# A gather of four experts for 32 tokens in a PEER layer, and two routers moved into the stretches with gathers

## The reference

```
q = (x @ wq).reshape(N, 8, 2, 128)                 # 8 heads
s = einsum('nhpd,hpkd->nhpk', q, keys)             # 128 keys a half
top_s, top_i = top_k(s, 16)                        # per half, then over all 16 x 16 sums
best_s, best = top_k(top_s[0] + top_s[1], 16)
expert = i1 * 128 + i2                             # 16 experts a head, 128 a token, of 16384
gate = softmax(best_s)
a = gelu(einsum('tkd,td->tk', u_tab[expert], x))
y = einsum('tk,tkd->td', gate * a, v_tab[expert])
```

## Time and profile before

| | |
|---|---|
| median of three runs | 5940.83 us |
| profiled execution | 5949.21 us, span 5947.1 us |
| busy: TensorE, VectorE, ScalarE, GpSimd | 4117.5, 2900.9, 1697.3, 1441.5 us |
| moved by DMA | 1712.65 MB, of it 1342.26 MB by GpSimd's queue |
| gathers | 1280 |
| matmul records of the sums (L774) | 10240, busy 1564.5 us |
| dots (L2020) | 1280, busy 1552.5 us |

### The profile page before, as it was taken

One profiled execution on the slowest core, in us unless ns is written; L12 is line 12 of the kernel. 1 busy time (PEld: TensorE's weight loads), 2 busy tenths in 40 slices (PEclk: granted clock), 3 DMA queues, 4 the chain that ended last, 5 costly groups with the idle time before them and its releaser, 6 DMA issues.

```text
span 5947.1 us, 63889 instructions
## 1 busy us (share of the span) xinstructions
PE 4117.5 (69%) x22248; PEld 2506.1 (42%) x22248; DVE 2900.9 (49%) x6835; ACT 1697.3 (29%) x4733; POOL 1441.5 (24%) x1295
## 2 busy tenths in 40 slices
PE   3889477889886685548476677778468785545555
PEld 1677454566563443224132235677335453211111
DVE  0321747544438544664445444322854445654444
ACT  0200137332432342233322222201152442222222
POOL 0000022212221232223343341000023332235443
PEclk7779789969997897778788888669778898767777
DMA  6434367748886798679999995024378997689998
GB/s 257 151 130 162 121 248 281 290 170 319 329 343 234 302 420 328 266 274 386 379 409 411 394 420 200 27 67 155 117 286 361 369 402 318 256 335 421 407 417 358
DMA packets 259315, 1712.65 MB, mean 288 GB/s; under 512 B 37712, under 2 KB 39344, under 8 KB 71600
## 3 DMA queue, kind: packets, MB, share of 16 engines
q0 software_dynamic: 184320, 1342.26, 56.4%
q1 hardware_dynamic: 74672, 366.31, 16.6%
HBM read 1690.43 MB, written 17.92 MB: 287 GB/s over the span
## 4 chain that ended last, share of the span: by engine, by line
PE 42%; DMA 24%; DVE 15%; ACT 6%; issue 4%; DVEq 4%; POOL 3%; ACTq 2%; SPq 1%; PEldq 0%; PEld 0%; POOLq 0%
PE psum L423 25%; DMA arena<-in_uv,arena 21%; PE psum L774 10%; DVE arena L2020 3%; POOL arena L1108 3%; DVE arena L1932 1%; DVE arena L1925 1%; DMA arena<-in_w_ada 1%; DVE arena L1926 1%; PE psum L383 1%; PE psum L604 1%; PE psum L605 1%; ACT arena L1444 1%; ACT arena L1441 1%; PE psum L639 1%
## 5 line engine op out<-in xcount | busy, mean ns | idle before, releaser
L1108 POOL DMA_INDIRECT arena<-in_uv,arena x1280 | 1437.6, 1123 | 4469.9 <-PE psum L774 3039.1
L774 PE MATMUL psum<-arena 64*64 64x512 f32 x10240 | 1564.5, 742 | 1086.5 <-ACTq L1445 990.9
L2020 DVE CUSTOM_DVE_ANT_0 arena<-arena 128x1024 f32<-128x1024 f32 x1280 | 1552.5, 1226 | 1330.0 <-DMA arena<-in_uv,arena 1272.4
L423 PE MATMUL psum<-arena 128*128 128x256 f32 (+2 forms) x8480 | 1945.9, 388 | 171.4 <-DVEq L1464 120.4
L423 PEld LDWEIGHTS psum<-arena 128*128 128x128 f32 (+1 forms) x8480 | 1616.9, 195 | 599.2 <-issue 194.1
L774 PEld LDWEIGHTS psum<-arena 64*64 64x64 f32 x10240 | 392.7, 157 | 2068.6 <-ACTq L1445 1375.8
L1438 ACT ACTIVATE arena<-arena 128x2 f32<-128x2 f32 x640 | 130.9, 205 | 1684.8 <-DVEq L2022 1671.3
L1444 ACT ACTIVATE arena<-arena 128x64 f32<-128x64 f32 x1280 | 376.2, 340 | 45.8 <-issue 1.8
L383 PE MATMUL psum<-arena 128*128 128x128 f32 (+1 forms) x680 | 129.4, 346 | 337.3 <-DVE arena L1523 119.8
L1441 ACT ACTIVATE arena<-arena 128x1 f32<-128x1 f32 x1280 | 307.6, 287 | 45.5 <-issue 1.3
L383 PEld LDWEIGHTS psum<-arena 128*128 128x128 f32 (+1 forms) x680 | 97.9, 178 | 391.2 <-issue 183.5
(11 more groups left out here) (210 smaller groups left out, 2747.4 us busy)
## 6 DMA issues: line engine op xcount, KB each, us to landing
arena<-in_w_in SPq DMA_DIRECT2D x92, 1024.0 KB, 5.9
arena<-in_w_mix SPq DMA_DIRECT2D x120, 768.0 KB, 7.3
arena<-in_w_ada SPq DMA_DIRECT2D x32, 1536.0 KB, 16.4
arena<-in_w_wq SPq DMA_DIRECT2D x40, 1152.0 KB, 6.0
arena<-in_w_wo SPq DMA_DIRECT2D x20, 1024.0 KB, 7.5
arena<-in_uv,arena POOLq DMA_INDIRECT x1280, 10.8
arena<-ada_rows SPq DMA_DIRECT2D x15, 512.0 KB, 5.6
arena<-x_rows SPq DMA_DIRECT2D x14, 512.0 KB, 6.2
```

The lines of the kernel that those rows point to most:

```text
L423: ins = mm(out, a, b, start=(i == 0), stop=(i == last))
L774: ins = mm(psum[o, r_ * 512:r_ * 512 + 512], DIAG[rows, c, :], RING[rows, sl, D + half * 512:D + (half + 1) * 512], start=first, stop=last ...
L1108: pool.indirect_dma_start(RING[:, sl, :], None, io["uv"], bass.IndirectOffsetOnAxis(IDX[:, t, h * TOPK + k:h * TOPK + k + 1], 0)).then_inc ...
L2020: V_.tensor_tensor_reduce(out=RING[:, sl, 0:D], in0=RING[:, sl, 0:D], in1=XT[:, u % 2, :], scale=1.0, scalar=0.0, op0=ALU.mult, op1=ALU.ad ...
```

## The change

A gather now brings, to partition 32e + i, an expert of token i of 32 tokens: four experts each (e = 0 to 3) for 32 tokens. A unit is half a tile, 64 tokens as two sets of 32, with 32 groups of two gathers; there are 20 units. Since the partitions no longer stand for tokens one by one, the picks of a head go through DRAM: VectorE writes numbers and gates to `PICK`, SyncE stores them to `pick_rows`, waits, and loads them in four pieces into `PICKED` (`hand_over`); GpSimd and ScalarE wait for `picked`. The token rows are loaded four times over into `XT`, one buffer for each set of 32, by ScalarE's queue. `QUAD`, four stacked 32x32 identities, takes the place of `PAIR`, and the sum has four matmuls of 128x32 and 256 columns, one for each quarter of the width, in two PSUM banks that alternate by unit. `route` of layer 0 pair 0 and of layer 1 pair 1 moves to the head of the next segment, with cost 28 a head, and `quotas` holds back items whose head isn't handed over.

```
-GROUPS = PH * TOPK // GS
+TG = 32
+SUB, PER = P // TG, TOPK * TG // P
+HG = 2 * PER // GS
+GROUPS = PH * HG
...
-        return [12.0] * PH
+        return [(28.0 if (l, pairs) in OVERLAPPED else 12.0)] * PH
-UNITS = [(0, t) for t in range(NT)] + [(1, t) for t in range(CT, NT)]
+OVERLAPPED = ((0, (0,)), (1, (1,)))
+UNITS = [(0, t, f) for t in range(NT) for f in range(2)] + [(1, t, f) for t in range(CT, NT) for f in range(2)]
...
+                if st[0] == "route" and n < PH - 1:
+                    want = max(done, min(want, routed_upto(items, st[1], st[2], n - 1)))
...
-        PAIR = view(keep(64), [64])
+        QUAD = view(keep(TG), [TG])
...
+        def acc_bank(u):
+            return psum[:, (u % 2) * 512:(u % 2) * 512 + 512]
...  TensorE
-                if g == 0 and u:
-                    pe.wait_ge(s("acc_out"), u)
+                if g == 0 and u >= 2:
+                    pe.wait_ge(s("acc_out"), u - 1)
-                    for half in range(2):
-                        for r_ in range(2):
-                            rows, o = slice(64 * r_, 64 * r_ + 64), slice(64 * (half ^ r_), 64 * (half ^ r_) + 64)
-                            ins = mm(psum[o, r_ * 512:r_ * 512 + 512], DIAG[rows, c, :], RING[rows, sl, D + half * 512:D + (half + 1) * 512],
+                    for q in range(4):
+                        ins = mm(acc_bank(u)[32 * q:32 * q + 32, gg * 256:gg * 256 + 256], DIAG[:, c, :], RING[:, sl, D + q * 256:D + (q + 1) * 256],
...  SyncE
+                def hand_over(h):
+                    n = PH * r + h
+                    sp.wait_ge(s("gated"), n + 1)
+                    rows = pick_rows[n]
+                    sp.dma_start(rows.rearrange("(t p) c -> p t c", p=P), PICK[:, h % 2]).then_inc(s("pick_out"), 16)
+                    sp.wait_ge(s("pick_out"), 16 * (n + 1))
+                    if n:
+                        sp.wait_ge(s("picked"), 64 * n)
...
+                    for e in range(4):
+                        src = rows[:, 2 * PER * e:2 * PER * (e + 1)].rearrange("(g p) c -> p g c", p=TG)
+                        sp.dma_start(PICKED[r % 2][TG * e:TG * (e + 1), h], src).then_inc(s("picked"), 16)
                 for h in range(PH):
                     chunks(1)
+                    if h:
+                        hand_over(h - 1)
+                    if h == PH - 1:
+                        hand_over(h)
                     yield
...  ScalarE
+            def load_xt(u, gg):
+                l, t, f = UNITS[u]
+                xt[gg] += 1
+                at_ = t * P + 64 * f + TG * gg
+                for e in range(4):
+                    act.dma_start(XT[TG * e:TG * (e + 1), gg, :], h2_rows[at_:at_ + TG, :]).then_inc(s(f"xt_in{gg}"), 16)
...
+                if u + 1 < len(UNITS) and (UNITS[u + 1][0], UNITS[u + 1][1] // 2) in h2_ready:
+                    if g == GROUPS - 1 - HG // 2:
+                        load_xt(u + 1, 0)
+                    if g == GROUPS - 1 and xt[1] == u + 1:
+                        load_xt(u + 1, 1)
```

More of the change, by code:

```diff
@@ L129, in schedule @@
+    e1 = [("route", 1, (1,)), ("q", 1, (2,)), ("da", 1, (2,)), ("ml_on", 1, both), ("mc", 1, (2,)), ("mln", 1, (2,)), ("merge", 1, (2,)), ("route", 1, (2,))]
+    p0 = sequence(range(0, 4))
+    p1 = sequence(range(4, 12))
+    p2 = sequence(range(12, 20))
+    cut = 4 * GROUPS
     return [(a, [], 0), (b, p0, 0), (c1, p1[:cut], 0), (c2, p1[cut:], 8), (d, [], 0), (e1, p2[:cut], 0),
-            ([("final", 2, ())], p2[cut:cut + GROUPS], 8), ([("final", 3, ())], p2[cut + GROUPS:cut + GROUPS + 16], 8),
@@ L131, in schedule, with routed_upto @@
-            ([("final", 4, ())], p2[cut + GROUPS + 16:], 16), ([("final", 5, ())], [], 0)]
+            ([("final", 2, ())], p2[cut:cut + 64], 8), ([("final", 3, ())], p2[cut + 64:cut + 80], 8),
+            ([("final", 4, ())], p2[cut + 80:], 16), ([("final", 5, ())], [], 0)]
 SEGMENTS = schedule()
 PSEQ = [item for _, items, _ in SEGMENTS for item in items]
+def routed_upto(items, l, pairs, heads):
+    for i, item in enumerate(items):
+        if item is not None:
+            (ul, t, _), g = UNITS[item[0]], item[1]
+            if (ul, (t // 2,)) == (l, pairs) and g // HG >= heads:
+                return i
+    return len(items)
@@ L145, in quotas @@
             row = []
-            for cost in steps(*st):
+            for n, cost in enumerate(steps(*st)):
                 cum += cost
                 want = lead + int(round((len(items) - lead) * cum / total))
+                if st[0] == "route" and n < PH - 1:
+                    want = max(done, min(want, routed_upto(items, st[1], st[2], n - 1)))
                 row.append(want - done)
@@ L351, in slots, with route_of, picked_by, picks @@
         def slots(u, g):
[L353 to L354 removed]
+            first = u * GROUPS * GS + g * GS
+            return [(n, n % RS, n % 16, g // HG, (g * GS + i) // PER % 2, (g * GS + i) % PER) for i, n in enumerate(range(first, first + GS))]
         ROUTES = [(l, pairs[0]) for stages, _, _ in SEGMENTS for kind, l, pairs in stages if kind == "route"]
[L358 to L360 removed]
+        def route_of(u):
+            l, t, _ = UNITS[u]
+            return ROUTES.index((l, t // 2))
+        def picked_by(u, h):
+            return 64 * (PH * route_of(u) + h + 1)
+        def picks(u, h, gg):
+            _, t, f = UNITS[u]
+            return route_of(u) % 2, h, 4 * (t % 2) + 2 * f + gg
+        def last_unit(l, t):
+            return UNITS.index((l, t, 1))
+        def acc_bank(u):
+            return psum[:, (u % 2) * 512:(u % 2) * 512 + 512]
+        def x_of(u, c):
+            _, t, f = UNITS[u]
+            return x_rows[t * P + 64 * f:t * P + 64 * f + 64, c * 256:(c + 1) * 256].rearrange("(g p) n -> p g n", g=2)
         ADA_IN = [view(DN + 3072 * i, [KD, ADA_W]) for i in range(8)]
@@ L1425, in final @@
                 yield
-            def group(i):
+            h2_ready = set()
+            xt = [0, 0]
+            def load_xt(u, gg):
+                l, t, f = UNITS[u]
+                xt[gg] += 1
+                at_ = t * P + 64 * f + TG * gg
+                for e in range(4):
+                    act.dma_start(XT[TG * e:TG * (e + 1), gg, :], h2_rows[at_:at_ + TG, :]).then_inc(s(f"xt_in{gg}"), 16)
+            def group(i):
+                ahead = PSEQ[i]
+                if ahead is not None and ahead[1] == 0:
+                    for gg in range(2):
+                        if xt[gg] <= ahead[0]:
+                            if ahead[0]:
+                                act.wait_ge(s("dots"), GROUPS * ahead[0])
+                            load_xt(ahead[0], gg)
                 item = PSEQ[i - LAG_ACT] if i >= LAG_ACT else None
```

151 lines of the change are left out of this document (70 added, 81 removed).

## The result

The changed kernel took 5986.39 us (median of four runs, 5982.49 to 5996.51) where the kernel before took 5942.73 beside it (5940.66 to 5944.63): ratio 1.0081, interval 1.0066 to 1.0096, so 0.8% slower where 0.7% faster was forecast. The profiled span is 5980.2 us.

What follows compares the result with a forecast made beforehand. Bounds: gather bytes in DMA-full stretches, TensorE in dense work from 753 to 1966, VectorE in routers without groups. Terms 133 + 213 - 140 - 217 - 39 + 5 + 5 - 3 = -43 gave 5906, as median 5898 us; range 5800 to 5990.

Steps and rivals of the forecast that it cites:

- the halved sums: Sums on TensorE: 0.86 us less a group, whole in dense stages, about a third in latency-bound, nothing in DMA-full ones.
- the second PSUM bank: At tile ends: TensorE no longer waits for VectorE to empty the sum, -10 us from 753 to 1966, smaller gains later.
- the copies: Token rows loaded four times over: 16 MB more, 2.5 us a MB where DMA is full.
- the move: Two routers moved into stretches with groups: +133 and +213 us there, some -256 in what they leave behind.
- late hand-overs: Ends of the other three routers: hand-overs make SyncE late for the next stage, +5 us.
- rival 2: Quicker sums bring nothing, since strips queue or the clock falls between shorter bursts: 6022 us; chance 0.08.
- the second row: From the first moved router to the end of pair 1's router: 30 groups fewer (-66) and quicker sums, together -140 us.
- The steady head: Moved routers, heads with four groups: 34.6 us less 1.5 for quicker sums, 33; trip plus gather, 28, fits in.
- Late weights behind the trip: Two bare heads of each moved router: SyncE issues head h+2's weights only behind a hand-over, +4 us (0 to 8).
- The stall at the single XT buffer: Token-row reloads no longer double-buffered: ring slots hide the first, the second stalls some 5 us once, +5.
- Rival 1: Routers: the trip through DRAM sets the head; at 43 us, ten heads lose 10 each, 5998 us; chance 0.20.
- Rival 3: Slots return sooner, TensorE no longer holds VectorE in routers: heads at 28 us, total 5788 us; chance 0.20.

Runs made afterwards that it cites:

- i1: Kernel before, with 256 in place of 512 columns in the sums of all but a unit's first and last gathers (part of the output wrong): 5895.80 us, ratio 0.9917.
- g4: New layout, routers not moved, weights issued early, one of four token-row copies reloaded (dots wrong): 5896.26 us, ratio 0.9917.
- f4: New layout with the routers not moved, SyncE issuing weights before it waits for the trip: 5973.39 us, ratio 1.0047.
- f3: Changed kernel, SyncE issuing weights before it waits for the trip: 5988.24 us, ratio 1.0075.
- e2: Kernel before with only the two routers moved, old layout, as many groups in each step as the changed kernel: 5980.89 us, ratio 1.0065.
- g1: Changed kernel with one of four token-row copies reloaded after the first unit (dots wrong), waits kept: 5927.66 us, ratio 0.9971.
- e4: Changed kernel with two idle matmuls ahead of the wait for each group's matrix, groups 8 to 31 of each unit: 5998.39 us, ratio 1.0103.
- f1: Changed kernel with token rows loaded for the first unit only (later dots wrong): 5907.17 us, ratio 0.9938.
- h2: New layout, routers not moved, weights early, token rows of 17 of 20 units loaded once and spread by TensorE and ScalarE: 5901.73 us, ratio 0.9925.
- f2: Changed kernel with one hand-over per router, 35 of 40 trips through DRAM left out (most experts wrong): 5983.80 us, ratio 1.0067.
- e1: Changed kernel with both routers back where they were, new layout kept: 5997.57 us, ratio 1.0090.
- e3: Changed kernel with each sum matmul issued twice and the result halved by VectorE: 6044.68 us, ratio 1.0168.

## Why the prediction was wrong

Put end to end, with each step between two runs, the change is: the halved sums -44 (i1), the rest of the new layout without extra copies 0 (g4 against i1), three more copies of the token rows +77 (f4 less g4), the move +15 (f3 less f4), late weights -2 (after less f3, which issues the weights early). That makes 46; 44 by the medians and 48 by the ratios were measured. In another order the shares differ: the move costs 40 on the kernel before (e2), and the copies 59 once it is made (g1). The forecast had the halved sums at -124, the second PSUM bank at -30, the copies at +25, the move at about +85 and late hand-overs at +5.

- **The step that failed first is the price of the halved sums**: 0.86 us a group "whole" in dense stages and a third of it in latency-bound ones, with the stage's own matmuls as fast as before. Measured are 44 to 58 us for 124. In the dense stages of layer 0 it held nearly (47 us for 51, the normalizations counted in). But in the mLSTM, where it put a gain, shorter sums left TensorE at the lower clock (0.52 for 0.68) and the stage grew by 22 us (20 in i1, gone again in e4): the prediction named a falling clock in rival 2, yet its sum has nothing for it. In the routers heads stayed at 34.5 us, since VectorE still waits 6.90 for queries that start after two cold groups and take 7.72; i1 shows 7 us for pair 2's router where 12 were forecast. In the merge of pair 2 i1 shows 1 us for 16: the forecast took the whole gap between the stage's 401 us and its DMA's 377 for gain, down to 385.
- **The token rows' DMA was too small.** Priced at 2.5 us a MB and in the DMA-full parts alone, 8 + 8 + 4 and a stall of 5. Measured 59 to 77 for 15 MB, and it is bytes (g1). The tail shows it plainly: forecast 3 less, came out 9 more, and f1 gives 19 back.
- **The second PSUM bank**, some 30 us in waits at unit ends, no run tried alone. Its waits are gone (87 us in 7 of them before, none after), but g4 with it and i1 without it take the same time, so either they cost nothing or something else of the new layout costs as much.
- **The move was right in its parts.** 282 and 370 us for forecasts of 290 and 373; the last stretch -231 for -217; merge 241 us for 256; and e2, with the groups moved and nothing else, takes 60 us less in the second row, for 66 forecast. Its net was forecast worse than it is. That it is a loss by itself stood in the prediction and holds (15 to 44 us), but the sums that were to pay for it bring too little.
- **The steady head** at 33 us came as 33.4 to 36 in the moved routers; the terms of the trip did not matter, since trip and gather, 5 + 12, take half a head.
- **Late weights behind the trip** were priced at 4 us for bare heads in the moved routers. That holds there (f3), but without the move they cost 24 us (f4).
- **The stall at the single XT buffer** shows nowhere in the changed kernel: VectorE's idle time before the dots ends with gathers, as before. With the routers not moved there are two or three waits for the rows, 27 us in f4 and 24 in h2, so they are no part of what separates these two.

**Rival 1** (slower, 5998) came nearest in time and is wrong in its mechanism: f2 takes 35 trips away for 3 us. **Rival 2** is wrong in that the sums bring nothing, for they bring 44 to 58 us and the strips don't queue; but the falling clock that it names is real and takes back 20 to 23 us in one stage. **Rival 3** fell: TensorE no longer waits for VectorE at a unit's end, and heads with four groups stand at 33 to 38 us, not at 28; only the last interval of each moved router is 27.4, and e2, with the old layout, has 28.5 there. The measured 5986 us lies inside the widest range, 5800 to 5990, by luck: its upper end was rival 1's trip, and what filled it were the token rows and the clock.

Open: of the 124 us, 64 were in the second row, where i1 gained 18, and 60 elsewhere, where it gained 37; why a group brings 0.53 to 0.74 us in dense stages and not 0.86, and next to nothing in attention, is not settled. Nor is it why the move costs less beside four copies. e1 closes: -44 + 77 + 24 make 57, and 57 were measured (54 by the ratios).

## What to carry to other kernels

Before a saving on an engine is counted, go through it stage by stage. Where TensorE runs dense matmuls back to back, most of the saving came; in one stage of short matmuls between waits, the thinner work cost it the clock and the stage got longer. A time summed over several stages hid both: 565 us in e3 and after. Doubling the work in question (one edit) gave its price in one run, 58 us for the 44 that halving brought. When a layout change multiplies a small operand, as here, its bytes go on the scarcest resource: price them by a measured rate of such transfers, and not in the full stretches alone, and look for an engine with time to make the copies on chip. A queue that works in order and gets a new wait should first issue what others need from it.

## What the runs showed of the hardware

- Four column strips over 128 rows, fp32, run together: 16 records of 256 columns in 1.07 us at the upper clock, 1.94 at the lower.
- Small pieces through DRAM and back are mostly quick: 1.6 us for the store and 1.8 for a load (medians; at most 9.3 and 24.8). The Trainium skill (DMA: Bandwidth & Descriptors, the table at its head) wants 512 B or more a piece for full rate. Here the pieces of at most 128 B of 35 trips took some 36 us of the 16 engines' time (SyncE's queue has 16.8% of the span in the kernel after, 16.2% in f2) and 3 us of run time; the prediction's estimate by that page was 62 us of DMA time for 40 trips.
- 128 KB loads of 4 KB rows took 3.7 us a MB of all 16 engines' time, the gathers of 8 KB rows 2.53. In run time they cost 3.9 to 5.2 us a MB (g1, and f4 less g4).
- Less work for TensorE lowers its granted clock (0.814 to 0.727 over the kernel; i1, with halved sums alone, 0.738), and its other matmuls then take longer: 408 us for 373 in one stretch. One stage of small matmuls, 170 us at 0.52, takes 148 at 0.67 or 0.68 (e2, e3). Matmuls thrown away raise the clock (0.788) and win those us back in that stage, and over the kernel they cost more than they bring (12 us).
